# Modulation sums through 32 columns of ones, and the last two output pieces block by block

## The reference

```python
c_act = jax.nn.silu(c)
mod = c_act @ mod_w + mod_b                     # 3 * 1024 columns per sublayer, K = 1024
h = rmsnorm(x, norm_g) * (1 + scale) + shift
x = x + 0.5 * (1 + gate) * swiglu(h, w_gu, w_down)    # sublayers 0 to 5
x = x + gate * rmsnorm(mixer(h), norm_g_2)            # sublayers 6 to 13
```

## Time and profile before

| | |
|---|---|
| median of 3 runs | 2340.66 us (2340.03 to 2340.7) |
| the profiled execution | 2336.99 us |
| its span, first to last instruction | 2335.1 us |
| mean granted TensorE clock | 0.98 |
| PE busy | 2157.7 us (92%) |
| DVE, ACT, POOL busy | 1598.3, 1199.1, 342.5 us |
| HBM read | 530.12 MB |

### The profile page before, as it was taken

One profiled execution on the slowest core, in us unless ns is written; L12 is line 12 of the kernel. 1 busy time (PEld: TensorE's weight loads), 2 busy tenths in 40 slices (PEclk: granted clock), 3 DMA queues, 4 the chain that ended last, 5 costly groups with the idle time before them and its releaser, 6 DMA issues.

```text
span 2335.1 us, 37968 instructions
## 1 busy us (share of the span) xinstructions
PE 2157.7 (92%) x14752; PEld 1958.7 (84%) x14752; DVE 1598.3 (68%) x1832; ACT 1199.1 (51%) x1840; POOL 342.5 (15%) x525
## 2 busy tenths in 40 slices
PE   2999998999999996999988999889997899998998
PEld 1998887998899894998876998858986898877987
DVE  6767765777776776776887776536766776665654
ACT  2554555644554465653565554536544554575543
POOL 0111100111121103121000220430211221000210
PEclk9999999999999998999999999999999999999999
DMA  8788883789887962798665677643778378442653
GB/s 338 249 312 308 288 304 110 267 291 329 268 310 270 300 229 56 261 322 288 236 241 171 212 279 270 186 113 116 261 287 243 98 254 289 148 138 73 198 190 108
DMA packets 298884, 537.79 MB, mean 230 GB/s; under 512 B 11250, under 2 KB 188925, under 8 KB 298749
## 3 DMA queue, kind: packets, MB, share of 16 engines
q1 hardware_dynamic: 263452, 358.05, 47.0%
q0 software_dynamic: 35296, 177.87, 21.6%
HBM read 530.12 MB, written 1.11 MB: 228 GB/s over the span
## 4 chain that ended last, share of the span: by engine, by line
PE 79%; DVE 8%; ACT 6%; issue 4%; DMA 3%; SPq 0%; POOL 0%; DVEq 0%; ACTq 0%
PE bk L1372 12%; PE bk L1373 12%; PE bk L1374 12%; PE bk L1273 9%; PE bk L1271 9%; PE bk L1272 9%; PE bk L1426 2%; DVE w_lo L1753 2%; DMA mod_raw<-in_ada_w 2%; PE bk L1259 1%; PE bk L1261 1%; PE bk L1260 1%; PE bk L1628 1%; DVE mod_acc L1772 1%; ACT w_hi L834 1%
## 5 line engine op out<-in xcount | busy, mean ns | idle before, releaser
L1753 DVE TENSOR_TENSOR w_lo<-raw,w_hi 128x1024 fp32r<-128x1024 f32 (+5 forms) x720 | 833.4, 1186 | 498.9 <-ACT w_hi L834 497.2
L834 ACT ACTIVATE w_hi<-raw 128x1024 fp32r<-128x1024 f32 (+5 forms) x720 | 683.3, 976 | 667.4 <-PE bk L1273 337.8
L1372 PE MATMUL bk<-a_hi,w_hi 128*128 128x256 f32 x2332 | 663.0, 284 | 9.6 <-DVE a_lo L1838 4.8
L1373 PE MATMUL bk<-a_lo,w_hi 128*128 128x256 f32 x2332 | 661.7, 284 | 0.0
L1374 PE MATMUL bk<-a_hi,w_lo 128*128 128x256 f32 x2332 | 661.6, 284 | 0.0
L1372 PEld LDWEIGHTS bk<-a_hi,w_hi 128*128 128x128 f32 x2332 | 449.5, 193 | 10.9 <-DVE wcols L2114 5.0
L1373 PEld LDWEIGHTS bk<-a_lo,w_hi 128*128 128x128 f32 x2332 | 449.5, 193 | 0.0
L1374 PEld LDWEIGHTS bk<-a_hi,w_lo 128*128 128x128 f32 x2332 | 449.4, 193 | 0.0
L1772 DVE SCALAR_TENSOR_TENSOR mod_acc<-mod_raw,cact,mod_acc 128x1536 f32<-128x1536 f32 x182 | 329.7, 1812 | 37.0 <-DMA mod_raw<-in_ada_w 23.5
L1271 PE MATMUL bk<-w_hi,hid_hi 128*128 128x512 f32 x832 | 324.1, 390 | 3.5 <-DVE w_lo L1753 3.2
L1273 PE MATMUL bk<-w_hi,hid_lo 128*128 128x512 f32 x832 | 327.3, 393 | 0.0
(11 more groups left out here) (346 smaller groups left out, 2973.7 us busy)
## 6 DMA issues: line engine op xcount, KB each, us to landing
raw<-in_ffn_w SPq DMA_DIRECT2D x128, 1024.0 KB, 5.7
mod_raw<-in_ada_w POOLq DMA_DIRECT2D x128, 768.0 KB, 6.2
raw<-in_ffn_w_gu SPq DMA_DIRECT2D x88, 1024.0 KB, 7.7
mod_raw<-in_mod_w POOLq DMA_DIRECT2D x80, 768.0 KB, 6.9
raw<-in_ffn_w_down SPq DMA_DIRECT2D x40, 1024.0 KB, 6.9
first_mod<-in_mod_w SPq DMA_DIRECT2D x16, 768.0 KB, 10.1
raw<-in_sb_w_qkv SPq DMA_DIRECT2D x12, 1024.0 KB, 7.4
raw<-in_conv_w_pw SPq DMA_DIRECT2D x12, 1024.0 KB, 5.8
```

The lines of the kernel that those rows point to most:

```text
L834: ins = act.activation(o(w_hi[:, p % OPS, :]), r(raw[:, c % RAWS, :]), ACT.Copy)
L1372: pe.matmul(o, wh, a_hi[:, f, :], start=(f == 0), stop=False)
L1373: pe.matmul(o, wh, a_lo[:, f, :], start=False, stop=False)
L1753: ins = dve.tensor_tensor(o(w_lo[:, p % OPS, :]), r(raw[:, c % RAWS, :]), o(w_hi[:, p % OPS, :].bitcast(F32)), ALU.subtract)
```

## The change

1. `mod_sum` becomes `mod_rows` and `mod_turn`. `mod_rows` has 6 matmuls: 32 columns of ones are the weights and 512 columns of `mod_acc` the moving side; they go to four column groups, so that sums lie as rows (32 equal ones) in the four 32-partition quarters of one bank and two quarters of the next. ACT copies these rows back into `mod_acc` (`mod_copy`: 128 x 512 and 64 x 512), and PE turns them with 8 transposes (`mod_turn`). DVE reads with two operations where one was.
2. In the ffn1 stream `mod_rows` stands behind q = 0 (was q = 1), `mod_turn` behind q = 2, ACT's copy between pieces p+36 and p+37.
3. At the start `mod_copy` stands on ACT behind the rope's sine, and DVE's `mod_finish` still ahead of the first four `w_lo`.
4. Late groups: behind ffn1 and sb, `mod_rows` is at the stage's start and the copy on ACT between the squares of block 0 and 1, together with a `w_hi` piece that is held back to there. Behind mla and ffn2, `mod_rows` stands between block 0 and block 1 of the last pieces. Then `keep_busy` with 6 and `mod_turn`.
5. `last_piece` becomes `last_pieces` with `HELD = 2`: the last two pieces are done for block 0, then both for block 1.
6. DVE makes one `w_lo` less ahead of the last outputs and one more behind the norms, ahead of `mod_finish` and the first `a_lo`. `post` is called for each block by itself, right behind that block's result. In mla the units stand one place earlier, in ffn2 the last ones too.

```diff
+            def mod_copy(w):
+
+                act.wait_ge(rows_done, k.next("rows") + 1)
+                act.activation(mod_acc[:, 0:512], bk[:, 4 * (w % 2), :], ACT.Copy)
+                act.activation(mod_acc[0:2 * Q, 512:1024], bk[0:2 * Q, 4 * (w % 2) + 1, :], ACT.Copy).then_inc(rows_out, 1)
...
                         tokens_inverse(2, 20, 9)
+                        pieces(held, held + 1)
+                        if rows is not None:
+                            mod_copy(rows)
...
                     act.activation(rope[NOPE:P, :], rs[NOPE:P, 0, :], ACT.Sin).then_inc(rope_ready, 1)
+                    mod_copy(1)
...
-            def job(c, w, i, xs, kt0, kts, ready, outs=None, tail=None):
+            def job(c, w, i, xs, kt0, kts, ready, outs=None, tail=None, rows=None):
 
                 is_free(pe, w, i)
                 n = (kts + 1) // 2
-                for q in range(n if tail is None else n - 1):
+                for q in range(n if tail is None else n - HELD):
                     piece(2 * c + q, i, ready, xs, kt0 + 2 * q, outs or by_feature(w), q == 0, q == n - 1)
                 if tail is not None:
-                    last_piece(2 * c + n - 1, w, xs, kt0 + 2 * n - 2)
-
-            def last_piece(p, w, xs, kt):
-
-                pe.wait_ge(lo_ready, 2 * RAWS + p + 1)
+                    last_pieces(2 * c + n - HELD, w, xs, kt0 + 2 * (n - HELD), rows)
+
+            def last_pieces(p0, w, xs, kt, rows):
+
                 for b, a, e in CUTS[2:]:
+                    if b and rows is not None:
+                        mod_rows(rows, w + 1)
                     o, s = y_bank(w, b, a, e), slice(P * b, P * b + P)
-                    for r in range(2):
-                        wh, wl = (z[:, p % OPS, 512 * r:512 * r + 512] for z in (w_hi, w_lo))
-                        xh, xl = (z(kt + r)[:, s] for z in xs)
-                        pe.matmul(o, xh, wh, start=False, stop=False)
-                        pe.matmul(o, xh, wl, start=False, stop=False)
-                        ins = pe.matmul(o, xl, wh, start=False, stop=(r == 1))
-                    if b == 0:
-                        ins.then_inc(tail_done, 1)
-                    else:
-                        ins.then_inc(piece_used, 2 if p in double else 1)
+                    for q in range(HELD):
+                        p = p0 + q
+                        if b == 0:
+                            pe.wait_ge(lo_ready, 2 * RAWS + p + 1)
+                        for r in range(2):
+                            wh, wl = (z[:, p % OPS, 512 * r:512 * r + 512] for z in (w_hi, w_lo))
+                            xh, xl = (z(kt + 2 * q + r)[:, s] for z in xs)
+                            pe.matmul(o, xh, wh, start=False, stop=False)
+                            pe.matmul(o, xh, wl, start=False, stop=False)
+                            ins = pe.matmul(o, xl, wh, start=False, stop=(q == HELD - 1 and r == 1))
+                        if b:
+                            ins.then_inc(piece_used, 2 if p in double else 1)
+                        elif q == HELD - 1:
+                            ins.then_inc(tail_done, 1)
...
-                    if second is not None and q == 1:
-                        second()
+                    if group is not None and q == 0:
+                        mod_rows(group, w + 1)
+                    if group is not None and q == 2:
+                        mod_turn(w + 1)
...
-            def mod_sum(g, w, a=0, b=MODC // P):
-
-                if a == 0:
+            def mod_rows(g, w):
+
+                if g:
                     is_free(pe, w)
-                    pe.wait_ge(mod_used, 2 + UNITS * (g + 1))
-                for j in range(a, b):
-                    ins = pe.matmul(mod_wide(w, j), mod_acc[:, P * j:P * j + P], one1[:, :], start=True, stop=True)
-                if b == MODC // P:
-                    ins.then_inc(turn_done, 1)
-                    k.add("turn", 1)
+                pe.wait_ge(mod_used, 2 + UNITS * (g + 1))
+                for c in range(MODC // 512):
+                    ins = pe.matmul(mod_row(w, c), one1[:, 0:Q], mod_acc[:, 512 * c:512 * c + 512], start=True, stop=True)
+                ins.then_inc(rows_done, 1)
+
+            def mod_turn(w):
+
+                pe.wait_ge(rows_out, k.next("rows") + 1)
+                for s in range(4):
+                    pe.transpose(mod_turned(w, 0, s), mod_acc[:, P * s:P * s + P], ident[:, :])
+                for s in range(4):
+                    ins = pe.transpose(mod_turned(w, 1, s), mod_acc[0:2 * Q, 512 + P * s:512 + P * s + P],
+                                       ident[0:2 * Q, 0:2 * Q])
+                ins.then_inc(turn_done, 1)
+                k.add("turn", 1)
...
-            mod_sum(0, 0)
+            mod_rows(0, 1)
+            mod_turn(1)
...
-                    mod_sum(st["late"], w)
+                    if after(g) in ("plain", "final"):
+                        mod_rows(st["late"], w)
+                    keep_busy(job_banks(w)[:, 3, :], 6)
+                    mod_turn(w)
...
-            def tokens_normed(g):
+            def tokens_normed(g, p):
...
+                if g and kinds[g - 1] != "pool":
+                    pieces(p + 1 + early(g), p + 2 + early(g))
...
-                    if kinds[g] not in POST:
+                    if kinds[g] in POST:
+                        post(g, i - 2)
+                    else:
                         added(g, i)
...
-                    pieces(p + 66, p + 67)
                     second_half(g, w + 9, c + 32)
-                    post(g)
...
-                    unit(13)
+                    unit(14)
                     pieces(p + 27, p + 28)
-                    unit(14)
+                    unit(15)
                     pieces(p + 28, p + 29)
-                    unit(15)
-                    pieces(p + 29, p + 31)
+                    pieces(p + 29, p + 30)
```

More of the change, by code:

```diff
@@ L47 @@
 UNITS = KD * MODC // MODW
+HELD = 2
 def param_rows(shapes):
@@ L958, in y_tail @@
                     tokens_inverse(i, 18 + i, 7 + i)
+                    if i == 2 and rows is not None:
+                        mod_copy(rows)
             def heads_out(n, bank=4):
@@ L990, in _ @@
                     x_squares()
+                    if kinds[g - 1] != "pool":
+                        pieces(p + 2, p + 3)
                 act.wait_ge(mod_ready, g + 1)
@@ L1013, in _ @@
                     y_first(g, w + 8, c + 24)
-                    pieces(p + 51, p + 67)
-                    y_tail(g, w + 8, c + 32)
+                    pieces(p + 51, p + 66)
+                    y_tail(g, w + 8, c + 32, w + 10 if st["groups"] else None)
                 elif st["kind"] == "mla":
@@ L1092, in _ @@
                     y_first(g, w + 10, c + 12)
-                    pieces(p + 27, p + 31)
-                    y_tail(g, w + 10, c + 14)
+                    pieces(p + 27, p + 30)
+                    y_tail(g, w + 10, c + 14, w + 12 if st["groups"] else None)
                 elif st["kind"] == "conv":
@@ L1352, in first_gate_up, with gate_up @@
                     ins.then_inc(piece_used, 1 + 2 * q)
-            def gate_up(c, w, i, second=None, act_from=None):
+            def gate_up(c, w, i, group=None, act_from=None):
                 is_free(pe, w, i)
@@ L1389, in mean, with ends @@
                 k.add("root", 1)
+            def ends(st):
+                return st["groups"][-1] if st["groups"] else None
             def y_mean(w):
@@ L1592, in _ @@
                     job(c + 10, w + 10, 0, A, 0, KD, None, by_token(w + 10))
-                    job(c + 12, w + 11, 0, A, 0, KD, None, by_token(w + 11), tail=True)
+                    job(c + 12, w + 11, 0, A, 0, KD, None, by_token(w + 11), tail=True, rows=ends(st))
                 elif st["kind"] == "conv":
@@ L1659, in _ @@
                     for b in range(8, 11):
-                        gate_up(c + 2 * b, w + b, 0, second=(lambda: mod_sum(st["groups"][0], w + 9)) if b == 8 else None)
+                        gate_up(c + 2 * b, w + b, 0, group=st["groups"][0] if b == 8 else None)
                         turned()
@@ L1954, in _ @@
                 .then_inc(rope_arg, 1)
-            mod_finish(0, 0)
+            mod_finish(0, 1)
             pieces(0, 2)
@@ L1987, in _ @@
                         if st["groups"]:
-                            mod_add(st["groups"][0], 4 + u // 2, u % 2)
+                            for v in ((8,), (9,), (10, 11), (12,), (13,), (14,), (15,), ())[u]:
+                                mod_add(st["groups"][0], v // 2, v % 2)
                         if u == 3:
@@ L2043, in _ @@
                     pieces(p + 12, p + 14)
-                    unit(2)
+                    unit(3)
                     pieces(p + 14, p + 16)
@@ L2153, in _ @@
                     first_half(g, w + 5, c + 10)
-                    pieces(p + 23, p + 27)
+                    pieces(p + 23, p + 26)
                     second_half(g, w + 6, c + 12)
```

(4 more changed lines are left out.)

78 lines of the change are left out of this document (44 added, 34 removed).

## The result

The changed kernel takes 2349.02 us (median of 6 runs, 2346.56 to 2350.75), the kernel before 2338.98 us (6 runs, 2336.95 to 2340.7). The ratio is 1.0039, with a 95% interval of 1.0028 to 1.005: 9 us slower, some 10 by the medians. The forecast was 2349.5 and +8.9.

What follows compares the result with a forecast made beforehand. PE holds 79% of the chain, nearly all weight streaming, which the change leaves alone. 8.5 - 1.6 - 3.0 - 1.4 = +2.5, clock +6.4, total +8.9 on 2340.66: 2349.5 us, range 2345.5 to 2354 (chance 0.50).

Steps and rivals of the forecast that it cites:

- The start, +8.5: Program start: ACT's copy stands behind two w_hi and the sine, so norms begin at 69.3 instead of 60.75, 8.5 us later.
- How long the sum is: New sum on PE: six matmuls in four overlapping column groups 1.8 us, eight transposes 0.95; 2.75 in place of 5.5 us.
- The stream, waits of 9.7: ffn1 stream, stages 0, 2, 3, 5: mod_rows one step earlier waits for DVE's product, 9.7 us together; net -1.6.
- The gain of 2.8 each: ffn1 stream: each of four sums costs PE 2.75 in place of 5.5 us, 11.3 us won together.
- The first wait: ffn1 stream, stage 0: q = 0 ends at 159.95 + 0.03, DVE's product at 162.80, so PE waits 2.9 us.
- The rival of a stream without stalls: ffn1 stream: DVE runs 3 us further ahead, all four waits and dips go; -7.2 us, 2333.5; chance 0.12.
- The clock, +6.4: PE loses its clock behind stalls: two dips and two half chances in the stream, +4.8; passages 7 to 8, 11 to 12, +0.8 each.
- my bracket: PE's idle time before losing the clock: behind 1.91 us it stayed 1.00, behind 2.67 us it was 0.51 for 3.2 us.
- The passages, -3.0: Between stages: small changes per passage, from -1.9 (6 to 7) and -1.7 (12 to 13) to +1.3 (5 to 6); sum -3.0 us.
- the end, -1.4: Program end: squares of block 0 start 1.4 us earlier, two of four post operations done before block 1 is ready; -1.4 us.
- mod_rows and the block-wise start cancel: Passages behind mla and ffn2: mod_rows takes 1.8 us, block 0 goes 1.4 earlier; +0.5 (7 to 8), +0.35 (11 to 12).
- Stage 6, -1.9: Passage 6 to 7: last unit ends some 3 us sooner, first a_lo at 1281.0 in place of 1282.90; -1.9 us.

Runs made afterwards that it cites:

- the other base: Old start and mod_rows behind q = 1 together (0.9952, -11.2 us), set against the changed kernel with mod_rows behind q = 1 alone (0.9983, -4.0 us).
- the run with q = 1: Changed kernel with mod_rows behind q = 1 again in the ffn1 stream, start as changed; 0.9983, -4.0 us against the kernel before.
- the filled stalls: Changed kernel with keep_busy of 10 matmuls of ones ahead of mod_rows behind q = 0; 1.0016, +3.7 us against the kernel before.
- with the old sum: Changed kernel with old sums everywhere, keeping block-wise last two pieces, post per block, moved w_lo, w_hi and units; 0.9927, -17 us against the kernel before.
- the run with the blocks alone: Kernel before with only the last two pieces block by block and post per block; old sums, no w_lo moved; 1.0022, +5.1 us.
- one held piece in place of two: Fastest version (old sum at start and in passages, new one behind q = 1, 0.9899) with HELD = 1; 0.9915, -19.9 us against the kernel before.

## Why the prediction was right

- **The start, +8.5:** 8.3 in the trace. The copies were at 61.30 to 62.37 for a forecast 61.1 to 62.2, mod_finish at 64.19 for 64.1, the norms at 69.17 for 69.3. Putting it back gave 10.0 and, from the other base, 7.2.
- **How long the sum is:** 1.91 us for a forecast 1.8, so the four column groups overlap, as the conv's rows said. Turning took 1.0 (0.95) at full clock.
- **The stream, waits of 9.7:** 9.2. The gain of 2.8 each stands: in the run with q = 1 the streams of stages 2, 3 and 5 are 2.4, 3.9 and 2.4 shorter than before, that of stage 0 only 0.9. The first wait was misread: the matmul at 159.95 lasts 0.28, so q = 0 ends at 160.23 and the wait is 2.6; it took 2.66. The rival of a stream without stalls fell: DVE was no further ahead.
- **The clock, +6.4:** the mechanism is shown by the filled stalls, three low stretches behind the four sums where two and two halves were forecast. Filling the waits gave back 5.4 us by the times, for a forecast 4.8. 1.86 us of idle time was enough once, though 1.91 had done nothing before, and the other wait of 1.86 us did nothing: the lower end of my bracket was no bound.
- **The passages, -3.0, and the end, -1.4:** this is the step that was right only as a sum. In the plain passages each place is within 0.5 us; the first a_lo of stage 3 even came 0.3 us earlier against the last output (7.4 us behind it, before 7.7) where 0.4 later was forecast. For those behind mla and ffn2 I wrote that mod_rows and the block-wise start cancel, and left it at that. Each is much larger: the blocks with the moved w_lo and units are worth 17 us by the times (12 in the trace), and the new sum costs 10 to 12. That the sum of the two came near the forecast is luck. I had costed 9 to 10 and 10 to 11 at 0; these passages are -1.7 and 0.0 in the changed kernel and -1.9 and +0.4 with the old sum. And I had named the moved w_lo as a small cost behind the norms, where most of the gain depends on it: the run with the blocks alone went the other way, and with one held piece in place of two the moved w_lo, the units and the post per block still brought 19.9 of 23.6 us.
- **Stage 6, -1.9:** -0.2. The passage itself gave what was forecast (-3.9 with 1.9 of mod_rows to set against it), the rest is one more low stretch of the clock in the attention part, 1.7 us.

In all, by parts: blocks and moved pieces -17, the new sum in the stream behind q = 1 -6.5, in the passages +10 to +12, at the start +7 to +10, one step too early in the stream +10 to +13. Taking the middle of each, that is +8, where +9 was measured. This is no separate test, as the parts are differences of the same runs: along one path from before to after they add up by themselves. The forecast's +8.9 for a measured 9.1 is closer than its terms: the start, the waits and the clock in the stream came out near what was written, the passages only in sum, and the two profiled executions are 13.3 us apart.

## What to carry to other kernels

In this kernel the cheaper operation was worth its price only where its engine had no gap. Before rewriting one, look for what stands right behind it, and if that is a wait for another engine, as behind the old sum in the passages, it is hidden already. When a result now has to pass through another engine's queue, its cost is its place in that queue (8.3 us at the start), not the copy's microsecond. And a slot that is freed later must be followed to whoever fills it: here to the w_lo that had to move with it.

## What the hardware showed that I had not expected

The same idle time does not always lose the clock. In stage 12 groups of transposes stand behind waits for ACT. This is the one with the longest wait, with a window of that time, first before, then after the change:

```profile
2107.43 0.85 PE L1585 MATMUL bk<-ident,mp 128*128 128x128 f32 x6 [2.25 <-ACT tmp L1088]
...
2107.40:2108.30 0.90, 0.87 (x8) 0.73 (x10) 0.67 (x3) 0.16 (x1) 0.00 (x0) 1.00 0.00 0
```

```profile
2121.04 1.51 PE L1636 MATMUL bk<-ident,mp 128*128 128x128 f32 x6 [2.26 <-ACT tmp L1112]
...
2121.00:2122.55 1.55, 1.51 (x8) 1.21 (x10) 1.31 (x6) 0.17 (x1) 0.00 (x0) 0.50 0.00 0
```

After 2.25 us idle they took 0.85 us at a granted clock of 1.00, after 2.26 us they took 1.51 at 0.50, and PE's matmuls just ahead of the wait are the same in both. The surplus of the profiled pair fits such differences: without the start and the end, the granted clock was at 1.2 GHz for 85 us before and for 113 us after. At full load 28 us of it would cost 14, and not all of it is at full load. Three such stretches are those behind the sums in the stream; what caused each of the others was not tested. The versions also scatter, the kernel before no less than the others: it went from 2335.93 to 2351.59 us in one session, the changed kernel with the old start from 2334.09 to 2347.7 in another.
